# Two joined two-layer models on one core, five places given another order: the first output's weights, the second layer's input store, a norm of the modulated layer, the first and the last differential items

## What is computed

```python
def first_block(...):                     # layers A (gated linear attention) and B (dilated attention)
    mem_n = rmsnorm(mem, mem_norm_w)
    for i in range(2):
        h = rmsnorm(x, norm_w[i])
        mix, q_mem, gate = mixer_i(h, w_in_i)
        mem_o = memory_attention(q_mem, mem_n, w_memkv[i])       # 4 heads of 64, 256 keys
        branch = concatenate([mix, mem_o], axis=-1) * silu(gate)
        x = x + branch @ w_out[i]
    return rmsnorm(x, final_norm_w)

def _layer(x, xc, ...):                   # second block, two modulated layers C0 and C1
    h = _rms(x, g_pre) * (1 + scale) + shift                     # 512 latent tokens
    hc = _rms(xc, g_pre) * (1 + mod_c[1]) + mod_c[0]             # 256 context tokens
    # h @ w_in gives neighbourhood, differential and convolution parts
    a_out = neighbourhood_attention(...)
    # differential attention, 4 heads, 128 queries at a time:
    #   w = softmax(q1 k1) - lam * softmax(q2 k2);  o = w @ v
    b_out = rms(o, subln_g) * (1 - lam_init)
    c_out = silu(layer_norm(conv31(a * sigmoid(b))))
    y = concatenate([a_out * silu(na_g), b_out * silu(df_g), c_out * silu(cv_g)]) @ w_out
    x = x + gate * _rms(y, g_post)        # in layer 0 the context tokens get the same
```

## Time and profile before

| what | us |
|---|---|
| median of 3 runs | 1789.06 |
| lowest and highest run | 1783.83 to 1790.07 |
| the profiled execution's own time | 1785.76 |
| its span, first to last instruction | 1783.9 |
| PE busy | 1671.2 (94%) |
| DVE busy | 944.8 (53%) |
| ACT busy | 640.4 (36%) |
| POOL busy | 182.3 (10%) |

### The profile page before, as it was taken

The page is one execution under the profiler, slowest core; times in us unless marked ns, Lnnn a source line. Parts: engine busy times, 40 slices in busy tenths (PEclk is TensorE's granted clock), DMA queues, the critical chain, the costliest instruction groups (busy, mean ns, idle before and its releaser), DMA issues.

```text
span 1783.9 us, 22816 instructions
## 1 busy us (share of the span) xinstructions
PE 1671.2 (94%) x8922; PEld 1299.7 (73%) x8922; DVE 944.8 (53%) x1675; ACT 640.4 (36%) x1226; POOL 182.3 (10%) x217
## 2 busy tenths in 40 slices
PE   7999988989999999998999999979989999997997
PEld 6966766877878888887887778845557877885553
DVE  1223172265655656566276868346664477763462
ACT  3255352233233323353223343244433135323341
POOL 4044323100000000011010000001010011000000
PEclk9998989999999999999999999979999999996799
DMA  7111152332654765353141220420003242121000
GB/s 270 50 58 59 28 209 100 97 84 73 181 159 115 162 182 145 132 119 112 36 159 43 54 72 1 154 71 1 12 25 89 95 129 66 62 95 71 1 12 36
DMA packets 171218, 161.34 MB, mean 90 GB/s; under 512 B 40342, under 2 KB 154248, under 8 KB 171080
## 3 DMA queue, kind: packets, MB, share of 16 engines
q1 hardware_dynamic: 151336, 124.87, 23.8%
q10 hardware_dynamic: 16928, 25.27, 4.6%
q0 software_dynamic: 2848, 9.74, 1.4%
HBM read 149.80 MB, written 11.18 MB: 90 GB/s over the span
## 4 chain that ended last, share of the span: by engine, by line
PE 76%; DVE 13%; ACT 4%; issue 3%; DMA 2%; POOL 1%; ACTq 0%; DVEq 0%; POOLq 0%
PE psum L2424 42%; PE psum L2395 12%; PE psum L2902 7%; PE psum L2453 6%; PE psum L2444 2%; DVE arena L1851 2%; PE psum L2573 2%; PE psum L2502 2%; DVE stat L2304 1%; PE psum L2483 1%; DVE wring_r L1928 1%; DMA arena<-in_ctx 1%; DVE arena L1830 1%; DVE arena L1827 1%; DVE psum L2253 1%
## 5 line engine op out<-in xcount | busy, mean ns | idle before, releaser
L2424 PE MATMUL psum<-hT_r,wring_r 128*128 128x512 f32 (+1 forms) x1760 | 594.0, 395 | 15.9 <-DVE arena_r L1957 8.2
L2424 PEld LDWEIGHTS psum<-hT_r,wring_r 128*128 128x128 f32 (+1 forms) x1760 | 330.5, 188 | 97.2 <-issue 21.8
L2424 PE MATMUL psum<-arena_r,wring_r 128*128 128x256 f32 (+2 forms) x1408 | 380.5, 337 | 5.9 <-DVE arena_r L1976 5.1
L1456 ACT ACTIVATE arena<-psum 128x512 f32<-128x512 f32 (+5 forms) x255 | 149.0, 612 | 466.7 <-PE psum L2424 270.0
L2424 PEld LDWEIGHTS psum<-arena_r,wring_r 128*128 128x128 f32 (+1 forms) x1408 | 228.2, 191 | 35.2 <-issue 7.5
L2395 PE MATMUL psum<-arena 128*128 128x96 f32 (+9 forms) x1460 | 236.7, 390 | 10.6 <-DVE arena L2051 5.2
L2395 PEld LDWEIGHTS psum<-arena 128*128 128x128 f32 (+5 forms) x1460 | 168.3, 201 | 76.1 <-issue 52.9
L2424 PE MATMUL psum<-arena_r 128*128 128x512 f32 (+2 forms) x688 | 212.4, 348 | 0.0
L2453 PE MATMUL psum<-ident,arena 128*128 128x128 f32 (+2 forms) x1028 | 139.7, 285 | 39.4 <-DVE arena L1830 7.8
L2424 PE MATMUL psum<-hT_r,arena_r 128*128 128x512 f32 (+1 forms) x416 | 165.4, 398 | 4.2 <-DVE wring_r L1928 3.7
L2453 PEld LDWEIGHTS psum<-ident,arena 128*128 128x128 f32 (+2 forms) x1028 | 119.5, 147 | 60.4 <-issue 20.8
(11 more groups left out here) (223 smaller groups left out, 1896.6 us busy)
## 6 DMA issues: line engine op xcount, KB each, us to landing
wring<-in_w_in_b SPq DMA_DIRECT2D x54, 512.0 KB, 6.0
arena<-in_w_mod ACTq DMA_DIRECT2D x16, 1536.0 KB, 7.8
wring<-in_w_in SPq DMA_DIRECT2D x16, 1536.0 KB, 6.8
wring<-in_w_out SPq DMA_DIRECT2D x8, 2048.0 KB, 10.5
wring<-in_w_in_a SPq DMA_DIRECT2D x5, 1536.0 KB, 6.7
arena<-x_dram SPq DMA_DIRECT2D x3, 2048.0 KB, 10.8
wring<-in_w_in SPq DMA_DIRECT2D x6, 1024.0 KB, 5.5
arena<-ebias_dram SPq DMA_DIRECT2D x144, 32.0 KB, 1.9
```

The lines of the kernel that those rows point to most:

```text
L1456: return nc.scalar.activation(out, in_, ACT.Copy, scale=scale)
L2424: ins_ = nc.tensor.matmul(b[0:hi.shape[2], 0:width], w[:, k], v[:, k], start=k + p == 0, stop=(k, p) == (KT - 1, 2))
```

## The change

1. **First output's weights.** The "wide" step of the first half stands ahead of gate 6 instead of behind it. Its load no longer waits for the memory query's product, only for gate 5, the last reader of its slot. The memory query's two rounded splits therefore go to two rooms in `arena` (columns 10240 and 11264) instead of the ring's tails.
2. **Second layer's input store.** The four stores to `x0_dram` are issued by SP, each when the tile's last addition is done, in front of the next two weight loads, instead of by POOL.
3. **A norm of the modulated layer.** The final norm and the "C0" norm of tile 2 leave ("wout", "B") and get a step "xf" of their own behind ("hcT", 0), on VectorE, ScalarE and POOL; on ScalarE only the square for "C0" moves.
4. **First differential items.** VectorE copies all six value tiles (before, ScalarE copied the even ones), and the first item's `diff_combine` goes ahead of the second item's maximum instead of behind it. The other items stay.
5. **Last differential items.** For the last tile the first pieces of both output halves come ahead of "oN" and "doT"; the halves use banks 4 and 5 and "doT" bank 6. Then follow "doT", the addition of the tile before, and the two second pieces.

The line in `late` is only written otherwise.

```diff
@@ schedule
     add("a" * 8, "mS", "A")
+    add("", "wide", "wout", "A", 0)
     add("a", "gate", "A", 6)
-    add("", "wide", "wout", "A", 0)
...
     add("vvvv", "hcT", 0)
+    add("", "xf")
     add("vv", "woutl", "B")
...
-                add("av"[t % 2], "dv", l, t)
+                add("v", "dv", l, t)
@@ diff_stage, the tail
     project()
+    for half in range(2):
+        add("", "yo", l, last, half, 0)
     add("", "oN", l, last)
-    projected(last)
+    add("v", "doT", l, last)
     add("", "yx", l, before)
-    project()
-    project()
+    add("a", "yo", l, last, 0, 1)
     if l == 0:
         add("", "nx", before)
-    project()
-    project()
+    add("a", "yo", l, last, 1, 1)
     add("", "yx", l, last)
@@ fixed_banks
-    if kind in ("doT", "yo"):
-        return (7,)
+    if kind == "doT":
+        return (6,) if key[2] == TT - 1 else (7,)
+    if kind == "yo":
+        return (4 + key[3],) if key[2] == TT - 1 else (7,)
@@ split_place, split_room
-                return (n + 3) % UNITS
+                key, g = split_list[n]
+                return WSLOTS + 1 + g if key == ("qm", "A") else (n + 3) % UNITS
...
-                return 28672
+                return (28672, 10240, 11264)[u]
@@ sync_items and SP
-                if name[:2] == ("wout", "A"):
-                    free = order_of[("qm", "A")]
...
+            items.append((order_of[("wout", "A")] - 0.5, "x0_save", None))
...
+                elif what == "x0_save":
+                    for t in range(TT):
+                        evacuated(sp, ("wout", "A"), out_jobs(("wout", "A")).index((t, 1)))
+                        sp.dma_start(x0_dram[t * P:(t + 1) * P], x[:, t]).then_inc(x0_saved, 16)
@@ POOL, ("wout", "A")
-                            evacuated(pool, key, out_jobs(key).index((t, 1)))
                             norm_roots("B", t)
-                            pool.dma_start(x0_dram[t * P:(t + 1) * P], x[:, t]).then_inc(x0_saved, 16)
@@ VectorE
+            def final_norm(t):
+                dve.wait_ge(rstd_ready, norm_no["F", t])
+                nc.vector.scalar_tensor_tensor(x[:, t], x[:, t], norms["F"][4][:, t:t + 1], fw,
+                                               ALU.mult, ALU.mult).then_inc(x_final, 1)
+                norm_scale("C0", t)
...
+                elif kind == "xf":
+                    final_norm(TT - 2)
...
+                            if t != TT - 2:
+                                final_norm(t)
...
+                    if (t, h) == diff_items(l)[1]:
+                        diff_combine(n - 1)
                     for i in range(2):
                         full(dve, key, i)
...
-                    if n > diff_at(l, *diff_items(l)[0]):
+                    if n > diff_at(l, *diff_items(l)[1]):
                         diff_combine(n - 1)
```

More of the change, by code:

```diff
@@ L418, in late @@
 def late(key):
-    return key[0] == "dv" or key[0] == "cvZ" or key in (("dX", 0, "q", 2), ("dX", 0, "q", 3))
+    return key[0] in ("dv", "cvZ") or key in (("dX", 0, "q", 2), ("dX", 0, "q", 3))
 def diff_tiles(l):
@@ L474, in diff_stage @@
     project()
+    for half in range(2):
+        add("", "yo", l, last, half, 0)
     add("", "oN", l, last)
-    projected(last)
+    add("v", "doT", l, last)
     add("", "yx", l, before)
-    project()
-    project()
+    add("a", "yo", l, last, 0, 1)
     if l == 0:
         add("", "nx", before)
-    project()
-    project()
+    add("a", "yo", l, last, 1, 1)
+    assert not todo
     add("", "yx", l, last)
@@ L975, in split_place_free @@
                 read_by_pe(eng, ("wout", "A"))
+                return
+            if split_list[n][0] == ("qm", "A"):
+                read_by_pe(eng, ("AA", GH - 1))
                 return
@@ L1209, in _ @@
                         last = chunks[arg - WSLOTS][3]
-                        if name[:2] == ("wout", "A"):
-                            read_by_pe(sp, ("qm", "A"))
                         if name[:2] == ("wout", "B"):
@@ L1392, in _ @@
                             norm_roots("F", t)
-                            norm_roots("C0", t)
+                            if t != TT - 2:
+                                norm_roots("C0", t)
+                elif kind == "xf":
+                    norm_roots("C0", TT - 2)
                 elif kind == "woutl":
@@ L1469, in squares_b @@
                     square("F", t)
-                    act.wait_ge(x_final, t + 1)
-                    square("C0", t)
+                    if t != TT - 2:
+                        act.wait_ge(x_final, t + 1)
+                        square("C0", t)
             def rows(r, src, n):
@@ L1642, in _ @@
                     squares_b(key)
+                elif kind == "xf":
+                    act.wait_ge(x_final, TT - 1)
+                    square("C0", TT - 2)
                 elif kind == "Bproj":
@@ L1719, in _ @@
                     free(move(dst, full(act, key, 0)[:, :].rearrange("p (h q) -> p h q", q=P)))
-                elif kind == "dv" and key[2] % 2 == 0:
-                    free(move(dv[:, key[2]], full(act, key, 0)[:, 0:384]))
                 elif kind == "nE":
@@ L2088, in _ @@
                         if ph == "B":
-                            dve.wait_ge(rstd_ready, norm_no["F", t])
-                            nc.vector.scalar_tensor_tensor(x[:, t], x[:, t], norms["F"][4][:, t:t + 1], fw,
-                                                           ALU.mult, ALU.mult).then_inc(x_final, 1)
-                            norm_scale("C0", t)
+                            if t != TT - 2:
+                                final_norm(t)
                         elif t:
@@ L2239, in _ @@
                 elif kind == "dv":
-                    if key[2] % 2:
-                        free(nc.vector.tensor_copy(dv[:, key[2]], full(dve, key, 0)[:, 0:384]))
+                    free(nc.vector.tensor_copy(dv[:, key[2]], full(dve, key, 0)[:, 0:384]))
                 elif kind == "nM":
@@ L2893, in _ @@
                     w = chunk(pe, ("yo", l, half))
+                    b = bank(("yo", l, t, half, 1), 0)
                     if piece == 0:
@@ L2901, in _ @@
                     for k in ((0, 1, 2, 6), (7, 3, 4, 5))[piece]:
-                        ins_ = nc.tensor.matmul(psum[:, 7], src[:, k, tt * P:(tt + 1) * P], w[:, k], start=k == 0, stop=k == 5)
+                        ins_ = nc.tensor.matmul(b, src[:, k, tt * P:(tt + 1) * P], w[:, k], start=k == 0, stop=k == 5)
                     if piece:
```

## The result

Four runs of the changed kernel gave 1763.8 to 1765.85 us, median 1765.7; beside them the kernel before gave 1777.33 to 1790.07, median 1786.44. The ratio is 0.9889, with a 95% interval of 0.9849 to 0.9929: a gain of 1.1%, clear of the noise, though under 2%. Timed once more the ratio was 0.9880 (0.9863 to 0.9896). The forecast was 1767 in a range of 1757 to 1776; it held. The profiled execution has a span of 1762.0 us against 1783.9, and TensorE is busy 1664.8 us where it was 1671.2.

The account below looks back on a forecast made before the run. TensorE, busy in 94% of the span, was taken as the bound, so only its waits and slow clock could be won. The terms sum to 20.6 us, giving 1765.2 or 1768.5; 1767 was taken, range 1757 to 1776.

Parts of the forecast that it names:

- Part 1: First output's weights: rounding ahead of gate 6 starts 1.8 us earlier, so TensorE goes on sooner; gain 1.8, bounds 1.5 and 5.0.
- the far bound of 5.0: Part 1's upper bound: the 16 products run at full instead of half clock and take half the time.
- Part 2: Second layer's input: store ahead of loads lands by about 302, then ScalarE's wait for the load counts; gain 2.8, bounds 2.1, 5.7.
- the bound of 2.1: Part 2's lower bound: the last store still takes 9.6 us, from 298.7.
- Part 3: Modulated layer: context keys start 4 us earlier, new wait of some 3 us behind them; gain 2.1, bounds 0.3 and 2.8.
- the lower bound: Part 3's bound of 0.3: the new wait costs a stretch at half clock, 1.8 us.
- Part 4: First differential items: value copies on VectorE shorten TensorE's wait, combination hides; gain 1.7 in layer 0, 2.4 in layer 1.
- Part 5: Last items: first output pieces fill the wait, one 1.3 us gap remains; gain 6.4 (bounds 4.7, 6.5) layer 0, 3.4 layer 1.
- The clock bonus: Rival, chance 0.13: shorter waits in parts 1 and 2 and layer 1's scores keep the clock up; 26 to 29 us, 1759.
- Given back: Rival, chance 0.11: second waits close behind hold the first four parts' gains; only 10 to 12 us remain, 1777.
- Slower by half clock in layer 0: Rival, chance 0.02: reordering drops TensorE to half clock in layer 0's differential attention; 50 us more of it would give 1793.
- doesn't do what it says: Rival, chance 0.05: early output pieces cannot start because of banks or late sums; 9.8 us go, 1777 is left.

Follow-up runs that it names:

- e11: The changed kernel itself, unedited, profiled and timed again: median 1764.78 us, 0.9880 of the kernel before; profiled span 1762.0 us.
- e2: Changed kernel, but SP issues the fourth store behind the two weight loads: store took 11.9 us, layer B's first product came 13.8 us after the last addition.
- e3: Changed kernel, but SP issues the two weight loads only after all four stores have landed: layer B's first product came 12.6 us behind the last addition.
- e10: Changed kernel, but tile 2's moved norm does its scaling behind tile 3's two additions on VectorE: first keys' product at 828.48 us against 833.24.
- e5: Changed kernel, but the first item's combination is behind the second item's maximum again: item 0's scores to transposes 13.34 us (layer 0), 16.54 (layer 1).
- e6: Changed kernel, but ScalarE copies the even value tiles again: item 0's scores to transposes 15.34 us (layer 0), 18.74 (layer 1).
- e4: Changed kernel, but ScalarE rounds the late load's gate weights behind the eight activations of the second layer's input: span 1756.7 us.
- e12: Changed kernel with four edits: late load's rounding moved, other convolution banks, second weight remainder later, norm interleaved: median 1743.2 us, 0.9763 of the kernel before.
- e1: Changed kernel with parts 1 and 3 put back as before: span 1770.0 us.
- e9: Changed kernel, but VectorE forms the second weight remainder behind the copies of the last probabilities: last addition of the first output at 292.97 us.

## Why the prediction was right, point by point

**The sum.** 20.6 forecast, 21.9 in the profiles, 20.7 between the medians. All seven waits, and what is late behind each, were named right; the sizes were off by up to 1.4 us, to both sides. That the sum came out within 1.3 us of the profiles is in part luck, since a term 1.2 too large and a clock term of 1.3 left out cancel. By the medians of e11's table the gains are 2.7, 1.8, 2.4, 1.0, 2.2, 6.9 and 3.8, together 20.8, where 1.8, 2.8, 2.1, 1.7, 2.4, 6.4 and 3.4 were forecast: errors of up to 1 us, which cancel as well.

**Part 1**: the shift was 1.84 against 1.8. The term left out was the clock: I gave the half clock over the products as the far bound of 5.0 and took none of it. It was 1.3 in this profile. In the ten profiles with this code the products took 5.08 to 6.56 us, 5.72 in the middle, so the clock gave 0 to 1.5 and part 1 is worth 1.9 to 3.4 from one execution to the next.

**Part 2**: this term was too large, 2.8 for 1.6. The landing (near 3 us) and the next late thing (ScalarE's wait for the load) were right. The mis-sized step is "the loads queue behind four issues, some 1.2 us": the issue came 1.1 us later against the last addition, as said, but the load then took 8.0 instead of 7.0. The store that I sent ahead is company for the load as well, which e2 and e3 show. A smaller slip: the 2.7 was rounded up for the hand-over, but VectorE starts 0.78 us behind ScalarE's first activation (304.79 to 305.57), where the sum had 0.6, so it should have gone down. The measured 1.6 lies nearer the bound of 2.1 than the forecast, but not by that bound's mechanism, since no store took 9.6 us. Between 0.8 and 2.7 us of gain were seen over the nine profiles with this code.

**Part 3**: 2.1 against 2.4. The new wait of "some 3 us" was 2.60 and the transposes ran partly at half clock, as in the lower bound, but they hid behind VectorE's copies: in e11 they took 2.40 us, TensorE then waited 1.27, and the first keys' product started 3.67 us behind their start in both. e10 shows the reason given: the moved norm's latency in front of tile 3's.

**Part 4**: 1.7 and 2.4 against 1.1 and 3.2; with the second profile 2.1 and 1.9. What does not move with the clock is smaller than either term: in layer 1 item 1's scores start 1.8 us sooner against item 0's (7.02 for 8.84, in every profile with the copies on VectorE), and in layer 0 the wait in front of the 14 transposes is 1.0 shorter (1.46 for 2.44). The other 1.4 of layer 1's 3.2 is one group of scores at full clock (1.56 for 2.93), seen in the first profile alone. The argument (only the copies count, the combination hides) holds by e5 and e6.

**Part 5**: 6.4 and 3.4 against 6.9 and 3.8. The one gap left is 1.3 us from transpose to products, as forecast. From TensorE's former stop to the end 15.2 us remain in either layer where I had 15.6: three pieces in a row take 10.49 us, not three times 3.6. The upper bound of 6.5 was too low by this. In layer 0, 1.6 us of the 6.9 are the half clock of before, which the sum had counted in. These are the two firmest terms: the tails repeat to 0.02 us.

**The rivals.** The clock bonus came in part: in part 1 and at layer 1's scores in this profile, not behind part 2's wait, where the clock stayed at 0.50 until about 310. The argument against it, that waits of over 3 us remain, held at part 2 (6.68 us); in part 1 (3.07) the clock was down when the products began and came back within them. The rival's premise, that shorter waits leave the clock up, held for e4 and e12 at layer B's start (1.26 and 1.27 us, clock 1.00) and not at part 1: with waits of 3.07, 2.53 and 0.83 us the 16 products took 5.23, 6.56 and 6.06 (after, e10, e12). "Given back" fell by e1. "Slower by half clock in layer 0" did not show, and "doesn't do what it says" fell by the tails, which kept one gap.

## What to carry to other kernels

When one wait is taken away, look at what the next late thing waits for in its engine's order: here an engine's place in line (ScalarE's rounding of a late load ahead of work that needed nothing of it) held more than the transfer that was cured. A transfer that must land early goes in front of the large ones: here a store took 3.3 us in front, and 9.6 and 11.9 behind them, from two different engines. Two results that take turns in one PSUM bank are a wait that no row names as such ("issue"), and separate banks took out some 3 us per tail (2.9 and 3.3) before any step was moved. Profile one code twice before a microsecond behind a wait is put down to an edit, and count the profiles of other edits in, wherever they leave a place alone.

## What the runs showed of the hardware that was not expected

- A store of 512 KB issued by SP lands in 2.6 us alone, in 3.3 just ahead of the two weight loads, and in 11.9 right behind them (e3, after, e2); from POOL it took 3.0 alone and 9.6 behind them (before). Issued behind them, its issue on SP took 1.98 us instead of 0.32; the two loads' issues took 1.52 us right behind a store and 0.99 to 1.01 otherwise.
- The places where TensorE's clock falls and rises around a wait are not set by the code alone. With identical code the 16 products of part 1 took 5.08 to 6.56 us in ten profiles. Item 1's scores in layer 1, behind the same wait of 1.80 us, took 1.56 and 2.84, and six of the value tiles' transposes with their neighbours (14 in one row) 3.17 and 2.02. The clock at which a stretch between 171 and 182 us ran made it 10.1 or 12.1 us long, in kernels that do not differ there.
- A wait in front of TensorE's work of 1.27 us left the clock at 1.00 (e12, layer B); one of 6.68 us at the same place was followed by some 4 us at 0.50. The length of the last wait does not decide it alone: behind 1.24 us (e9) and 0.83 us (e12) the 16 products began at 0.50.
